# One stage in place of two: the first output projection also norms, turns and splits its rows

## The reference, cut to what matters

```python
def hybrid_layer(x, norm_g, w_in, ...):
    p = rmsnorm(x, norm_g) @ w_in
    ...
    y = jnp.concatenate([y_rwkv, y_attn], axis=-1) @ w_out
    return x + y

def first_block(x, ...):
    ...
    return rmsnorm(x, final_g)

def second_block(x, positions, mix_norm, w_in, ...):
    for l in range(DEPTH_2):
        h = _rmsnorm(x, mix_norm[l])
        proj = h @ w_in[l]
        ...
        x = x + jnp.concatenate([a, r], axis=-1) @ w_out[l]
        ...
```

## Time and profile before

| | |
|---|---|
| median of 3 runs | 5482.45 us (5482.18 to 5483.88) |
| profiled execution, its own time | 5489.44 us |
| its span, first to last instruction | 5487.8 us |
| TensorE busy | 5087.9 us, 93% |
| weight loads busy | 4381.8 us, 80% |
| VectorE busy | 2684.1 us, 49% |
| ScalarE busy | 2122.8 us, 39% |
| mean granted clock of TensorE | 0.958 |

### The profile page before, as it was taken

One profiled execution on the slowest core, in us unless ns is written; L12 is line 12 of the kernel. 1 busy time (PEld: TensorE's weight loads), 2 busy tenths in 40 slices (PEclk: granted clock), 3 DMA queues, 4 the chain that ended last, 5 costly groups with the idle time before them and its releaser, 6 DMA issues. The chain is left out here.

```text
span 5487.8 us, 92211 instructions
## 1 busy us (share of the span) xinstructions
PE 5087.9 (93%) x35964; PEld 4381.8 (80%) x35965; DVE 2684.1 (49%) x4393; ACT 2122.8 (39%) x3344; POOL 379.5 (7%) x613
## 2 busy tenths in 40 slices
PE   7996989979999999997989979999999999999994
PEld 5674977767777788886877768999999999999994
DVE  2497545431844655432165434444445555555444
ACT  2354236332444333322244523333334444444432
POOL 0121100000500100000032001000000000000001
PEclk8996999989999999998999989999999999999997
DMA  2110000221001223452100535444444555555544
GB/s 82 39 66 22 0 22 16 89 88 39 4 20 70 101 72 92 140 175 80 39 16 20 157 120 171 159 166 161 166 159 180 187 197 190 194 201 184 187 151 192
DMA packets 111616, 605.60 MB, mean 110 GB/s; under 512 B 13504, under 2 KB 17488, under 8 KB 81872
## 3 DMA queue, kind: packets, MB, share of 16 engines
q1 hardware_dynamic: 95360, 550.61, 28.5%
q0 software_dynamic: 12368, 38.97, 1.9%
q10 hardware_dynamic: 3712, 13.63, 0.6%
HBM read 533.54 MB, written 69.63 MB: 110 GB/s over the span
## 5 line engine op out<-in xcount | busy, mean ns | idle before, releaser
L3417 DVE TENSOR_TENSOR experts_low<-experts_raw,experts_high 128x1024 fp32r<-128x1024 f32 x678 | 810.4, 1223 | 958.6 <-ACT experts_high L3344 958.5
L3260 PE MATMUL ps<-experts_xs_high,experts_high 128*128 128x256 f32 (+1 forms) x3584 | 1032.3, 288 | 22.1 <-ACT experts_silu L3370 10.6
L3260 PE MATMUL ps<-experts_xs_low,experts_high 128*128 128x256 f32 (+1 forms) x3584 | 1030.6, 288 | 0.0
L3260 PE MATMUL ps<-experts_xs_high,experts_low 128*128 128x256 f32 (+1 forms) x3584 | 1030.6, 288 | 0.0
L3344 ACT ACTIVATE experts_high<-experts_raw 128x1024 fp32r<-128x1024 f32 x678 | 687.8, 1049 | 44.7 <-DMA experts_raw<-experts 44.4
L3260 PEld LDWEIGHTS ps<-experts_xs_high,experts_high 128*128 128x128 f32 x3584 | 675.1, 188 | 33.7 <-issue 25.2
L3260 PEld LDWEIGHTS ps<-experts_xs_low,experts_high 128*128 128x128 f32 x3584 | 675.4, 188 | 8.2
L3260 PEld LDWEIGHTS ps<-experts_xs_high,experts_low 128*128 128x128 f32 x3584 | 675.2, 188 | 0.0
L3252 PE MATMUL ps<-experts_high,experts_hid_high 128*128 128x512 f32 x1120 | 438.5, 392 | 0.0
L3252 PE MATMUL ps<-experts_low,experts_hid_high 128*128 128x512 f32 x1120 | 437.2, 390 | 0.0
L2904 PE MATMUL ps<-dense_x_parts,dense_w_parts 128*128 128x512 f32 x1848 | 423.9, 391 | 1.8 <-DVE dense_w_parts L3036 1.8
(11 more groups left out here) (569 smaller groups left out, 8759.5 us busy)
## 6 DMA issues: line engine op xcount, KB each, us to landing
experts_raw<-experts SPq DMA_DIRECT2D x226, 1536.0 KB, 6.3
dense_raw<-dense SPq DMA_DIRECT2D x46, 512.0 KB, 4.0
mixT<-dense SPq DMA_DIRECT2D x42, 512.0 KB, 3.9
mixT<-w_in SPq DMA_DIRECT2D x36, 512.0 KB, 3.5
y_slot<-mla_blank SPq DMA_DIRECT2D x15, 1152.0 KB, 20.0
out_proj_raw<-w_out SPq DMA_DIRECT2D x48, 256.0 KB, 2.8
proj_keys_raw<-w_in SPq DMA_DIRECT2D x20, 512.0 KB, 3.5
y_slot<-experts_y ACTq DMA_DIRECT2D x8, 1024.0 KB, 9.2
```

Of the source, the lines that this page charges most:

```text
L3260: last = nc.tensor.matmul(ps[:, m, 0:width], w[:, u, m, c], x[:, k, 0:width], start=(k == 0 and i == 0), stop=(k == KD - 1 and i == 2))
L3417: nc.vector.tensor_tensor(low[:, v, t, :], raw[:, v % NR, t, :], high[:, v, t, :].bitcast(F32), ALU.subtract).then_inc(split, 1)
```

## The change

out_proj becomes a function of its own, product_norms_and_turn, and the stage mix_norm0 goes for layer 0. Behind the scaling of row block b that goes to x_block, the new stage sums the squares of the scaled row (square_next), makes a second mean, root and reciprocal, scales by the next layer's gain into one of four buffers (scale_next), turns it (turn), and writes the high part (place) and the low part (lower) of the turned block. These go into x_high and x_low, the split operand of out_proj itself, in the 128 columns that product(b) was the last to read. They stay on chip and are the operand of proj0. The first two weight blocks of proj0 are loaded in the new stage too. To make room, mixT is allocated once for the whole program and takes over 8 of the 20 blocks of the tensor big; the functions that used big take the parts as front and big. The shapes of their instructions are the same.

```diff
+def product_norms_and_turn(core, name, operand, spare, weights, source, gain_row, normed, next_gain_row, xT, moves):
...
+            for n in range(2 * K):
...
+                if n == 1:
+                    sp.dma_start(gain, gain_row.to_broadcast([P, D])).then_inc(gain_in, 16)
+                    sp.dma_start(next_gain, next_gain_row.to_broadcast([P, D])).then_inc(next_gain_in, 16)
...
+            for b in range(NT):
+                sp.wait_ge(scaled, b + 1)
+                sp.dma_start(normed[b * P:(b + 1) * P, :], x[:, b, :]).then_inc(stored[min(b, 2)], 16)
+                if b == 4:
+                    sp.wait_ge(stored[0], 16)
+                    sp.wait_ge(stored[1], 16)
+                    sp.wait_ge(next_scaled, 2)
+                    for to, origin in moves:
+                        sp.dma_start(to, origin).then_inc(beside, 16)
+            sp.wait_ge(beside, 16 * len(moves))
+            sp.wait_ge(stored[2], 16 * (NT - 2))
...
+            def turn(b):
+                pe.wait_ge(next_scaled, b + 1)
+                if b == 0:
+                    pe.wait_ge(added, NT)
+                if b >= 2:
+                    pe.wait_ge(lowered, b - 1)
+                for k in range(KD):
+                    last = nc.tensor.transpose(turn_bank(b)[:, k, :], ready[b % 4][:, k * P:(k + 1) * P], core.c("eye"))
+                last.then_inc(turned, 1)
...
+            for b in range(NT):
+                if b < 3:
+                    pe.wait_ge(added, BANKS[b] + 1)
+                else:
+                    pe.wait_ge(added, NT + b - 2)
+                for k in range(K):
+                    if b == 0:
+                        pe.wait_ge(split, K + k + 1)
+                    last = three(BANKS[b % 3], k, b)
+                last.then_inc(product, 1)
+                if b >= 1:
+                    turn(b - 1)
+            turn(NT - 1)
...
+            for b in range(NT):
+                if b >= 2:
+                    place(b - 2)
+                square(1, b)
+                if b >= 1:
+                    take_next_root(b - 1)
+                take_root(b)
+                square_next(b)
+            take_next_root(NT - 1)
+            place(NT - 2)
+            place(NT - 1)
...
+            def add(h, b):
+                dve.wait_ge(product, h * NT + b + 1)
...
+            def scale_next(b):
+                dve.wait_ge(next_inverse, b + 1)
+                dve.wait_ge(scaled, b + 1)
+                if b >= 4:
+                    dve.wait_ge(turned, b - 3)
+                nc.vector.scalar_tensor_tensor(ready[b % 4], x[:, b, :], one(9, b), next_gain, ALU.mult, ALU.mult).then_inc(next_scaled, 1)
...
+            for b in range(NT):
+                add(1, b)
+                if b >= 2:
+                    lower(b - 2)
+                if b >= 1:
+                    average_next(b - 1)
+                average(b)
+                if b >= 1:
+                    invert_next(b - 1)
+                invert(b)
+                if b >= 1:
+                    scale_next(b - 1)
+                scale(b)
+            average_next(NT - 1)
+            lower(NT - 2)
+            invert_next(NT - 1)
+            scale_next(NT - 1)
+            lower(NT - 1)
+    st.end()
...
-def mix_layer(core, l, table, source, out, dump, then=None):
+def mix_layer(core, l, table, mixT, source, out, dump, xT=None, turned=None, then=None):
...
-                xT = split_tensors(core, s3, f"xT{l}", [P, KD, T])
-                norm_transpose(core, f"mix_norm{l}", as_rows(qk[:, :, :, :].rearrange("p a j n -> p (a j) n")), xT, f"mix_row{l}", source,
-                               room=mixT[:, 2:7, :], moves=[(mixT[:, u, :], d[f"w_in{l}"][u]) for u in range(2)])
+                if xT is None:
+                    xT = split_tensors(core, s3, f"xT{l}", [P, KD, T])
+                    norm_transpose(core, f"mix_norm{l}", as_rows(qk[:, :, :, :].rearrange("p a j n -> p (a j) n")), xT, f"mix_row{l}", source,
+                                   room=mixT[:, 2:7, :], moves=[(mixT[:, u, :], d[f"w_in{l}"][u]) for u in range(2)])
...
-        product_and_norm(core, "out_proj", flat[:, 0:8, :], d["w_out"], d["x"], d["final_g"], d["x_block"])
...
+        product_norms_and_turn(core, "out_proj", mixT[:, :, :], flat, d["w_out"], d["x"], d["final_g"], d["x_block"], d["mix_row0"], xT,
+                               [(mixT[:, u, :], d["w_in0"][u]) for u in range(2)])
```

More of the change, by code:

```diff
@@ L427, in projections, with rwkv_operands @@
     st.end()
-def rwkv_operands(core, big, small, decay_end, bonus, rate, cum):
+def rwkv_operands(core, front, big, small, decay_end, bonus, rate, cum):
     nc, d = core.nc, core.dram
@@ L439, in rwkv_operands @@
     length = st.sb("length", [P, 3, 8 * NT])
-    R, K, V, KK, A = big[:, 1], big[:, 3], big[:, 4], big[:, 0], big[:, 2]
+    R, K, V, KK, A = front[:, 1], big[:, 1], big[:, 2], front[:, 0], big[:, 0]
     two = lambda j: core.ps[:, 2 * j:2 * j + 2, :].rearrange("p b n -> p (b n)")
@@ L630, in rwkv_operands, with rwkv_chunks @@
     st.end()
-def rwkv_chunks(core, big, decay_end, moves):
+def rwkv_chunks(core, front, big, decay_end, moves):
     nc = core.nc
@@ L703, in fetch @@
                     core.settle(pool)
-                nc.gpsimd.tensor_copy(inp[:, u, 2:5, :, :], big[:, 2:5, :, cols]).then_inc(s["fetched"], 1)
+                nc.gpsimd.tensor_copy(inp[:, u, 2:5, :, :], big[:, 0:3, :, cols]).then_inc(s["fetched"], 1)
                 if later(n, 2):
@@ L707, in fetch @@
                     core.settle(pool)
-                nc.gpsimd.tensor_copy(inp[:, u, 0:2, :, :], big[:, 0:2, :, cols]).then_inc(s["fetched"], 1)
+                nc.gpsimd.tensor_copy(inp[:, u, 0:2, :, :], front[:, 0:2, :, cols]).then_inc(s["fetched"], 1)
                 if later(n, 1):
@@ L716, in query @@
                     core.settle(pool)
-                nc.gpsimd.tensor_copy(rq[:, :, :], big[:, 1, :, bass.ds(m * CH, CH)]).then_inc(s["query_in"], 1)
+                nc.gpsimd.tensor_copy(rq[:, :, :], front[:, 1, :, bass.ds(m * CH, CH)]).then_inc(s["query_in"], 1)
             fetch(0, 0, 0)
@@ L885, in store @@
                     act.wait_ge(s["y_ready"], m + 1)
-                    copy(big[:, 1, :, bass.ds(m * CH, CH)], wide(ROWS)).then_inc(s["y_copied"], 1)
+                    copy(front[:, 1, :, bass.ds(m * CH, CH)], wide(ROWS)).then_inc(s["y_copied"], 1)
                 if m is not None:
@@ L982, in rwkv_chunks, with rwkv_output_and_queries @@
     st.end()
-def rwkv_output_and_queries(core, big, gate, bonus, out, queries, latent_T, latent, w_uv, q_abs):
+def rwkv_output_and_queries(core, front, big, gate, bonus, out, queries, latent_T, latent, w_uv, q_abs):
     nc, d = core.nc, core.dram
     st = Stage(core, "rwkv_out")
-    dev, sq, Y = big[:, 2], big[:, 3], big[:, 1]
+    dev, sq, Y = big[:, 0], big[:, 1], front[:, 1]
     stat = st.sb("stat", [P, 3, 8 * NT])
@@ L3537, in build @@
         core = Core(nc, dram, ctx)
[L3538 to L3543, removed]
+        with nc.sbuf_tensor("mixT", [P, 8, T], F32) as mixT, ExitStack() as turned:
+            xT = first_block(core, mixT, turned, dump)
+            with nc.sbuf_tensor("rope_table", [P, T], F32) as table:
+                mix_layer(core, 0, table, mixT, dram["x_block"], dram["x_mixed0"], dump, xT, turned,
+                          then=lambda rows: dense_products(core, "dense", rows, dram["dense"], dram["hidden"], dram["x_mixed0"], dram["x_ffn"]))
+                mix_layer(core, 1, table, mixT, dram["x_ffn"], dram["x_mixed1"], dump)
+        expert_ffn(core, dram["x_mixed1"], dram["out"])
 def expert_ffn(core, source, out):
@@ L3584, in mix_layer @@
                 inputs_and_gates(core, f"inputs{l}", l, xT, d[f"w_hi{l}"], inputs, qk, z, mixT[:, 0:4, :])
+            if turned is not None:
+                turned.close()
             log_decays = sb2("log_decays", [P, NT, HALF])
@@ L3612, in as_rows, with first_block @@
     return x.rearrange("p a n -> p (a n)").rearrange("p (b n) -> p b n", b=NT)
-def first_block(core, dump):
+def first_block(core, mixT, turned, dump):
     nc, d = core.nc, core.dram
-    with nc.sbuf_tensor("big", [P, 5, 4, T], F32) as big:
+    front = mixT[:, :, :].rearrange("p (a j) n -> p a j n", a=2)
+    with nc.sbuf_tensor("big", [P, 3, 4, T], F32) as big:
         flat = big[:, :, :, :].rearrange("p a j n -> p (a j) n")
         with nc.sbuf_tensor("masks", [P, offset(NT) - offset(TOPK // P)], F32) as masks, nc.sbuf_tensor("small", [P, T], F32) as small:
-            down, queries, relu = flat[:, 0:4, :], flat[:, 8:10, :], flat[:, 10:12, :]
+            down, queries, relu = mixT[:, 0:4, :], flat[:, 0:2, :], flat[:, 2:4, :]
             with nc.sbuf_tensor("index_weight", [P, NT, IDX_HEADS], F32) as weight, ExitStack() as s2:
                 xT = split_tensors(core, s2, "xT", [P, KD, T])
-                norm_transpose(core, "norm_in", as_rows(flat[:, 0:8, :]), xT, "norm_row", d["x"], eye=d["constants"][:, 0:P],
```

(12 more changed lines are left out.)

137 lines of the change are left out of this document (129 added, 8 removed).

## The result

The changed kernel takes **5508.93 us** (5504.20 to 5516.43, 5 runs) against 5482.83 (5482.18 to 5484.88, 5 runs): ratio 1.0049, 95% interval 1.0038 to 1.0060. It is 26.1 us slower. Forecast were slower, +14.6, and 5485 to 5505: the direction holds, the time lies outside the range.

The account below looks back on a forecast made before the run. TensorE, busy 93% of the span, sets the pace, with the gap at the out_proj seam. Loop waits +24.4 and +6.2, removed stage -23.2, clock +7.2 give +14.6 on 5482.45: 5497 us, range 5485 to 5505.

Parts of the forecast that it names:

- The moves of tensors between names: Tensors renamed or reallocated by the edit: no instruction changes shape, costed at nothing, 1 us allowed either way.
- The waits: In out_proj's loop, transposes wait for scale_next behind VectorE's add: 5.0 us once, 3.73 five times.
- a run behind E(7): From the end of row block 7's second-half product in out_proj to proj0's first matmul: 17.5 us.
- the loop from E(1) to E(7): Ends of out_proj's second-half products, row blocks 1 to 7: longer by 30.6 us at full clock, +6.2 and +24.4.
- The clock: TensorE's clock falls after six waits in out_proj's loop: 1.2 us each, +7.2, bounds 0 and 10.2.
- Rival 1: TensorE's clock stays up through the loop's waits: +7.4, 5490 us, within 0.2%; chance 0.22.
- the bound of 10.2: Upper bound in us for clock falls in out_proj's loop: six waits, at most 1.7 each.
- Rival 2: In out_proj's loop the next product runs while transposes wait: -16, 5466 us, faster; chance 0.05.
- The removed stage: mix_norm0's loads, barrier and norm go between out_proj's last product and proj0: 17.5 instead of 40.7 us, -23.2.

Follow-up runs that it names:

- aligned: The changed kernel with 32 bytes of padding in front of first_xT, so its parts start at multiples of 64 bytes; 5498.60 us, ratio 1.0030.
- later_turn: The changed kernel with first_xT padded by 32 bytes and TensorE's transposes, with place and lower, one block later; 5460.00 us, ratio 0.9963.
- filled: The changed kernel with first_xT padded by 32 bytes, plus 12 unneeded matmuls before each wait for transposes but the last; 5485.88 us, ratio 1.0013.

## Why the prediction was wrong

- **What failed is one term.** "The moves of tensors between names change no shape of an instruction; I allow 1 us either way." No shape changed, but an address did. Measured: 10 to 11 us by the runs (aligned). From the distances of matmuls, at 6.5 ns each, it is 5.6 in proj0 (864 matmuls), 1.2 in inputs0 (192) and 2.5 in out_proj (384), together some 9. The two profiled proj0 stages differ by 3.9 only, since the execution of before ran part of it at a lower clock (0.97 and 0.98 in 1230 to 1290, where after has 1.00). With the address mended (aligned) the time is 5498.6, inside the range. That it is 1.6 from the forecast is in part luck: against the kernel before on its chip it is +18.5, for the +14.6 forecast.
- **A difference of spans that fits by chance.** The spans differ by 15.3, where 14.6 was forecast, and the medians by 26.1. The execution profiled for before reached out_proj 8.7 us later than that of after, in stages whose work is the same; measured from a common start the difference is 24.0. The steps of the sum are to be compared stage by stage.
- **The waits: right.** Forecast 5.0 once and 3.73 five times, a run behind E(7) of 17.5; measured 4.53, 3.73 six times (the one behind E(7) included), and 17.8. The work itself was right too: without the clock the loop from E(1) to E(7) grew by 30.7, forecast 30.6, though some 0.9 of the 30.7 is the address. The waits are what makes the change slow: with later_turn, which leaves VectorE's order of add and scale_next, the loop has none and the kernel is faster than before. So the place of the transposes in TensorE's list, not the amount of work, sets the time.
- **The clock: right in kind, its size right by some luck.** +7.2 for six waits; taken from the steps of the profiled execution (10.4 once, 11.8 to 12.0 four times, and 7.95 instead of 6.69 from the first transposes to E(2)) 7.2 as well, but as 1.3 to 1.6 us behind five waits and none behind the sixth. Other executions lose more: aligned and filled differ by 9.6 in the loop, where all six runs behind a wait in aligned had a mean clock of 0.70 to 0.82, and filled still has a fall behind its first wait. Rival 1, a clock that stays up, is out. The Trainium skill (TensorE: Matmul & The Clock Gate, HAM oscillation) lets each gap throttle anew; by it the bound of 10.2 was due. The traces agree for all six waits in aligned and for five of six in the changed kernel.
- **Rival 2** (matmuls behind a waiting transpose could run) is out: TensorE waited for every one, and the next product began only behind the transposes. The Trainium skill (same page, Step-by-step: what each phase is for) keeps matmuls in program order; the trace agrees with its eight waits in the waits view.
- **The removed stage: right.** -22.9 measured behind E(7), -23.2 forecast. With the waits and the address mended, this gain, less the time of the transposes (steps of 6.33 for 5.44), is what is left: the seam of later_turn is 19.0 shorter than that of before, and its median 21 lower.
- Open: why operands that start 32 bytes apart cost 6.5 ns a matmul, 1 to 2 us of aligned's gain, which is no more than the medians vary, and why the start of out_proj varies by some us from one execution to the next in kernels whose first part is the same.

## What to carry to other kernels

Work that is put into a loop of the busiest engine must be ready when its turn in that engine's list comes: look in which step the producing engine makes it, and put the consumer one step later rather than reorder the producer. A wait of some 4 us there cost itself and, on top, 1.2 to 1.6 us of clock (7.2 and 9.6 us over six waits). When an edit moves a tensor, compare the start addresses of the two operands of each matmul, modulo 64, with each other; and compare the same stages of two traces from a common start, not by their spans alone.

## What the runs showed of the hardware

A float32r matmul of 128x512 between loads of 128x128 takes 227 ns when both operands start alike modulo 64 bytes, and 233 ns when they start 32 bytes apart modulo 64: xT0 off 11.20 us for 48, weights off 11.20, both off 10.88, none off 10.88. It holds whichever of the two is moved. Only a distance of 32 bytes was tried.

The experts fit this, in the kernels before and after alike. Their second product (line 3252 of the kernel before, 128x512) has both operands 32 bytes beside a multiple of 64, and its matmuls start 227 ns apart in the trace of before. Their first product (line 3260, 10752 matmuls of 256 or 288 columns) has its weights 32 bytes beside one and its other operand on one. No run here moved either, so whether it is slowed, and by how much, is not shown; by the address alone it is the next place to try the padding.
